# Gate and up products of a feed-forward layer: a 512-column matmul over both halves of the activations, the halves summed by VectorE

## The reference

```python
D_FF = 2816
def swiglu(u, w_gu, w_down):                 # u 256 x 1024, w_gu 1024 x 5632, w_down 2816 x 1024
    gate, up = jnp.split(u @ w_gu, 2, axis=-1)
    return (jax.nn.silu(gate) * up) @ w_down
...
        u = rmsnorm(x, ffn_pre_g[i])
        x = x + rmsnorm(swiglu(u, ffn_w_gu[i], ffn_w_down[i]), ffn_post_g[i])
```

## Time and profile before

| | us |
|---|---|
| median of 3 runs (960.03 to 960.82) | 960.06 |
| the profiled execution, its own time | 959.71 |
| its span, first to last instruction | 957.9 |
| PE busy in the span | 925.8 |
| DVE busy in the span | 568.7 |
| ACT busy in the span | 482.9 |
| granted TensorE clock, mean (1 is 2.4 GHz) | 0.989 |

### The profile page before, as it was taken

One profiled execution on the slowest core, in us unless ns is written; L12 is line 12 of the kernel. 1 busy time (PEld: TensorE's weight loads), 2 busy tenths in 40 slices (PEclk: granted clock), 3 DMA queues, 4 the chain that ended last, 5 costly groups with the idle time before them and its releaser, 6 DMA issues.

```text
span 957.9 us, 15627 instructions
## 1 busy us (share of the span) xinstructions
PE 925.8 (97%) x6624; PEld 858.1 (90%) x6624; DVE 568.7 (59%) x645; ACT 482.9 (50%) x654; POOL 55.2 (6%) x67
## 2 busy tenths in 40 slices
PE   8999999999999989999999999999999599999996
PEld 7999998878898889999988999987998499999885
DVE  6788466895755655554543854665844745554533
ACT  6566467763645554444434644666544544444332
POOL 1000003450000000000000220000000000000000
PEclk9999999999999999999999999999999799999999
DMA  8856444235642565555555796424652355555551
GB/s 264 267 189 190 144 148 138 90 91 193 207 169 88 180 204 187 175 175 178 191 202 176 238 271 207 132 100 132 222 172 91 110 167 184 175 175 178 201 192 44
DMA packets 121061, 163.80 MB, mean 171 GB/s; under 512 B 4076, under 2 KB 106916, under 8 KB 121012
## 3 DMA queue, kind: packets, MB, share of 16 engines
q1 hardware_dynamic: 117684, 151.99, 49.0%
q0 software_dynamic: 3328, 11.10, 3.8%
HBM read 162.01 MB, written 1.07 MB: 170 GB/s over the span
## 4 chain that ended last, share of the span: by engine, by line
PE 83%; DVE 10%; ACT 4%; issue 2%; DMA 1%; SPq 0%; DVEq 0%; POOL 0%; ACTq 0%; POOLq 0%
PE bank L449 75%; DVE w_lo L1148 2%; DVE ntmp L1211 1%; PE bank L756 1%; PE bank L727 1%; DVE x L1214 1%; DVE ntmp L1190 1%; ACT ntmp L867 1%; PE bank L645 1%; PE bank L551 1%; DMA d_pair<-in_ssm_d_dram 1%; DVE stats L1179 1%; DVE stats L1181 1%; PE bank L811 1%; DMA pre_row<-in_kv_norm_g_dram 1%
## 5 line engine op out<-in xcount | busy, mean ns | idle before, releaser
L1148 DVE TENSOR_TENSOR w_lo<-w_raw,w_hi 128x2048 fp32r<-128x2048 f32 x135 | 309.1, 2294 | 215.2 <-ACT w_hi L845 215.1
L449 PE MATMUL bank<-actT_hi,w_hi 128*128 128x256 f32 x1280 | 365.5, 286 | 3.6 <-DVE actT_lo L1198 1.6
L449 PE MATMUL bank<-actT_lo,w_hi 128*128 128x256 f32 x1280 | 363.8, 284 | 0.0
L449 PE MATMUL bank<-actT_hi,w_lo 128*128 128x256 f32 x1280 | 363.7, 284 | 0.0
L845 ACT ACTIVATE w_hi<-w_raw 128x2048 fp32r<-128x2048 f32 x135 | 256.7, 1907 | 94.7 <-DMA w_raw<-in_ffn_w_down_dram 52.8
L449 PEld LDWEIGHTS bank<-actT_hi,w_hi 128*128 128x128 f32 x1280 | 246.9, 193 | 5.8 <-issue 5.0
L449 PEld LDWEIGHTS bank<-actT_lo,w_hi 128*128 128x128 f32 x1280 | 246.9, 193 | 0.1
L449 PEld LDWEIGHTS bank<-actT_hi,w_lo 128*128 128x128 f32 x1280 | 246.9, 193 | 0.0
L449 PE MATMUL bank<-w_hi,hT_hi 128*128 128x512 f32 x176 | 68.6, 390 | 0.0
L449 PE MATMUL bank<-w_lo,hT_hi 128*128 128x512 f32 x176 | 68.6, 390 | 0.0
L449 PE MATMUL bank<-w_hi,hT_lo 128*128 128x512 f32 x176 | 68.5, 389 | 0.0
(11 more groups left out here) (209 smaller groups left out, 1293.1 us busy)
## 6 DMA issues: line engine op xcount, KB each, us to landing
w_raw<-in_ffn_w_gu_dram SPq DMA_DIRECT2D x44, 1024.0 KB, 5.1
w_raw<-in_ffn_w_down_dram SPq DMA_DIRECT2D x22, 1024.0 KB, 4.9
w_raw<-in_ssm_w_in_dram SPq DMA_DIRECT2D x20, 1024.0 KB, 5.4
w_raw<-in_mem_w_kv_dram SPq DMA_DIRECT2D x16, 1024.0 KB, 5.5
w_raw<-in_ssm_w_out_dram SPq DMA_DIRECT2D x8, 1024.0 KB, 5.0
w_raw<-in_mem_w_q_dram SPq DMA_DIRECT2D x8, 1024.0 KB, 5.4
w_raw<-in_mem_w_o_dram SPq DMA_DIRECT2D x8, 1024.0 KB, 5.0
w_raw<-in_w_kv_dram SPq DMA_DIRECT2D x8, 1024.0 KB, 5.6
```

The costliest lines, as they stand in the source:

```text
L449: ins = pe.matmul(dst, a, b, start=first and n == 0, stop=last and n == len(passes) - 1, skip_group_check=True)
L1148: dve.tensor_tensor(lo[:, s, :], raw[:, s, :], hi[:, s, :].bitcast(F32), ALU.subtract).then_inc(w_lo_done, 1)
```

## The change

- `actT_hi` and `actT_lo` become the two planes of one tensor `actT` [128, 8, 2, 256], so that for each k the high and the low half lie side by side.
- PE: gate and up units go through a new `pair_unit`. For each c and k it issues one matmul of 512 columns (high weights with both halves of `actT[k]`) and one of 256 columns (low weights with the high half), the latter added onto columns 256 to 511. Each c has a bank of its own: columns 0 to 255 hold hi·hi, columns 256 to 511 hold hi·lo + lo·hi. Units alternate between banks 0, 1 and banks 2, 3.
- DVE: for every unit a `tensor_reduce` reads the two banks (1024 values on each partition, viewed so that the two halves of an output are the inner dimension, 256 values apart) and writes 512 sums, to `gate` for an even unit and to `hval` for an odd one. It frees the banks. The multiplication by gate then reads and writes `hval` in SBUF.
- ACT: silu reads `gate` in SBUF, in place, after DVE's sum (new semaphore `gate_ready` tells DVE); the copy to `hT_hi` waits for `h_ready`. `w_hi` is made for unit j+3, and one unit more is split ahead of the first pass.

```diff
     if name in ("gu0", "gu1"):
-        return "dve" if i % 2 else "act"
+        return "dve"
...
-        actT_hi = place("actT_hi", [P, KD, S], F32R)
-        actT_lo = place("actT_lo", [P, KD, S], F32R)
+        actT = place("actT", [P, KD, 2, S], F32R)
+        actT_hi, actT_lo = actT[:, :, 0, :], actT[:, :, 1, :]
...
+            def pair_unit(slot, b):
+
+                for c in range(2):
+                    for k in range(KD):
+                        cols = slice(k * TC + c * P, k * TC + (c + 1) * P)
+                        wh, wl = hi[:, slot, cols], lo[:, slot, cols]
+                        pe.matmul(bank[:, b + c, :], wh, actT[:, k].rearrange("p e n -> p (e n)"), start=k == 0, stop=False,
+                                  skip_group_check=True)
+                        ins = pe.matmul(bank[:, b + c, S:2 * S], wl, actT_hi[:, k, :], start=False, stop=k == KD - 1,
+                                        skip_group_check=True)
+                return ins
...
                 with pe.Fori(0, iters) as i:
                     for j in range(5):
                         if j:
-                            e, n = free_of_slot(j, i)
-                            pe.wait_ge(t_out[e], n)
+                            pe.wait_ge(t_out["dve"], i * 4 + (d0 + j - 1))
                         if j < 4:
                             pe.wait_ge(w_lo_done, i * 4 + (u0 + j + 1))
-                            t_unit((u0 + j) % SLOTS, (v0 + j) % 2, actT_hi, actT_lo).then_inc(w_used, 1)
+                            pair_unit((u0 + j) % SLOTS, j % 2 * 2).then_inc(w_used, 1)
...
 # ScalarE
-                    hi_unit(u0 + 2 + j, i, per)
-                    act.wait_ge(w_used, i * 4 + (u0 + j + 1) if per else u0 + j + 1)
+                    hi_unit(u0 + 3 + j, i, per)
                     if j % 2 == 0:
-                        act.activation(gate[:, j // 2 % 2], tiles((v0 + j) % 2), ACT.Silu).then_inc(t_out["act"], 1)
+                        act.wait_ge(t_out["dve"], i * 4 + (d0 + j + 1) if per else d0 + j + 1)
+                        act.activation(gate[:, j // 2 % 2], gate[:, j // 2 % 2], ACT.Silu).then_inc(gate_ready, 1)
                     else:
-                        act.wait_ge(t_out["dve"], i * 2 + (d0 + j // 2 + 1) if per else d0 + j // 2 + 1)
+                        act.wait_ge(h_ready, i * 2 + (g0 + j // 2 + 1) if per else g0 + j // 2 + 1)
                         act.activation(hT_hi[:, tile, :], hval[:, j // 2 % 2], ACT.Copy).then_inc(h_hi, 1)
...
-            hi_upto(U[("gu0", 0)] + 1)
+            hi_upto(U[("gu0", 0)] + 2)
...
 # VectorE
                     lo_unit(u0 + 2 + j, i, per)
+                    b = j // 2 % 2
+                    halves = bank[:, j % 2 * 2:j % 2 * 2 + 2, :].rearrange("p c (e n) -> p c n e", e=2)
+                    dst = hval if j % 2 else gate
+                    dve.wait_ge(w_used, i * 4 + (u0 + j + 1) if per else u0 + j + 1)
+                    dve.tensor_reduce(dst[:, b], halves, AX.X, ALU.add).then_inc(t_out["dve"], 1)
                     if j % 2:
-                        b = j // 2 % 2
-                        dve.wait_ge(w_used, i * 4 + (u0 + j + 1) if per else u0 + j + 1)
-                        dve.wait_ge(t_out["act"], i * 2 + (a0 + j // 2 + 1) if per else a0 + j // 2 + 1)
-                        dve.tensor_tensor(hval[:, b], tiles((v0 + j) % 2), gate[:, b], ALU.mult).then_inc(t_out["dve"], 1)
+                        dve.wait_ge(t_out["dve"], i * 4 + (d0 + j + 1) if per else d0 + j + 1)
+                        dve.wait_ge(gate_ready, i * 2 + (h0 + j // 2 + 1) if per else h0 + j // 2 + 1)
+                        dve.tensor_tensor(hval[:, b], hval[:, b], gate[:, b], ALU.mult).then_inc(h_ready, 1)
                         dve.wait_ge(h_hi, i * 2 + (h0 + j // 2 + 1) if per else h0 + j // 2 + 1)
                         dve.tensor_tensor(hT_lo[:, tile, :], hval[:, b], hT_hi[:, tile, :].bitcast(F32), ALU.subtract).then_inc(h_lo, 1)
```

More of the change, by code:

```diff
@@ L307, in program @@
         h_hi, h_lo = sem("h_hi"), sem("h_lo")
+        gate_ready, h_ready = sem("gate_ready"), sem("h_ready")
         stored = sem("stored")
@@ L480, in banked @@
                 pe.wait_ge(w_lo_done, u + 1)
+                if name in ("gu0", "gu1"):
+                    pair_unit(u % SLOTS, i % 2 * 2).then_inc(w_used, 1)
+                    return
                 f = t_unit if KIND[name] == "T" else v_unit
@@ L498, in fill_half, with loop_t @@
                     ins.then_inc(w_used, 1)
-            def loop_t(name, iters, free_of_slot):
+            def loop_t(name, iters):
                 u0, v0 = U[(name, 0)], V_OF[(name, 0)]
+                d0 = FREED[v0][1] - 1
                 for e, n in FREED[v0 - 2:v0]:
@@ L765, in feed_forward @@
                 name = f"gu{layer}"
-                a0, d0 = FREED[V_OF[(name, 0)]][1] - 1, FREED[V_OF[(name, 1)]][1] - 1
-                loop_t(name, 5, lambda j, i: (("act", "dve")[j % 2], i * 2 + ((a0, d0)[j % 2] + j // 2)))
+                loop_t(name, 5)
                 for i in (20, 21):
@@ L1060, in feed_forward @@
                 u0, v0 = U[(name, 0)], V_OF[(name, 0)]
-                a0, d0 = FREED[v0][1] - 1, FREED[v0 + 1][1] - 1
+                d0, g0 = FREED[v0][1] - 1, (FT // 2) * layer
                 act.preload_act_table_set("silu_and_others")
                 def unit(j, i, per, tile):
-                    hi_unit(u0 + 2 + j, i, per)
-                    act.wait_ge(w_used, i * 4 + (u0 + j + 1) if per else u0 + j + 1)
+                    hi_unit(u0 + 3 + j, i, per)
                     if j % 2 == 0:
-                        act.activation(gate[:, j // 2 % 2], tiles((v0 + j) % 2), ACT.Silu).then_inc(t_out["act"], 1)
+                        act.wait_ge(t_out["dve"], i * 4 + (d0 + j + 1) if per else d0 + j + 1)
+                        act.activation(gate[:, j // 2 % 2], gate[:, j // 2 % 2], ACT.Silu).then_inc(gate_ready, 1)
                     else:
-                        act.wait_ge(t_out["dve"], i * 2 + (d0 + j // 2 + 1) if per else d0 + j // 2 + 1)
+                        act.wait_ge(h_ready, i * 2 + (g0 + j // 2 + 1) if per else g0 + j // 2 + 1)
                         act.activation(hT_hi[:, tile, :], hval[:, j // 2 % 2], ACT.Copy).then_inc(h_hi, 1)
@@ L1078, in feed_forward @@
                     unit(j, 0, 0, slice(FT - 2, FT))
-                done[0] = u0 + 24
+                done[0] = u0 + 25
                 m_part(f"down{layer}")
@@ L1133, in _ @@
             turn(7, actT_hi)
-            hi_upto(U[("gu1", 0)] + 1)
+            hi_upto(U[("gu1", 0)] + 2)
             feed_forward(1)
@@ L1403, in feed_forward @@
                 name = f"gu{layer}"
-                u0, v0 = U[(name, 0)], V_OF[(name, 0)]
-                a0 = FREED[v0][1] - 1
+                u0 = U[(name, 0)]
+                d0 = FREED[V_OF[(name, 0)]][1] - 1
                 h0 = (FT // 2) * layer
```

## The result

The changed kernel takes 955.02 us, the median of 5 runs (952.92 to 955.59), against 960.03 us before (959.69 to 960.82). The ratio is 0.9945, with a 95% interval of 0.9935 to 0.9956: faster by 0.55%. The forecast was 950.7 us with a range of 948.8 to 954.5, so the direction held and the size didn't: 5.0 us came where 9.3 were expected, and the median lies outside the range. The profiled execution (954.65 us) has a span of 952.8 us, 5.1 less than before.

What follows compares the result with a forecast made beforehand. PE's matmul stream in the two feed-forward layers was taken as the bound. From 959.71 us, 9.3 us of PE saving (9.4 less 0.1 at low clock) gave 950.4, plus 0.35 to the median: 950.7 us, range 948.8 to 954.5.

Steps and rivals of the forecast that it cites:

- The bound: Both feed-forward layers: PE's own stream sets the time, number of matmuls times distance between starts; PE waits for nothing.
- The cost of a matmul: Gate and up units: 13.3 ns beside the columns at either width; one 512 for two 256 saves 13.4 ns, 9.4 us over 704 steps.
- The bounds for this term: PE's saving per gate and up step: not under 0, at most 26.7 ns if the 256-column matmul's 13.3 ns hid too.
- the 357 from which the prediction called itself wrong: Gate and up stretch: a distance of 357 ns or more between 512-column matmuls would prove the prediction wrong; 346.6 expected.
- Rival 1: PE's gate and up steps: less of the fixed part is saved, 2.5 ns a step, 1.8 us in all: 958.3 us; chance 0.03.
- Rival 3: Layer edges: late loads or ACT splits, or a sum of 1.6 to 2.1 us, make PE wait: 953 to 956 us; chance 0.06.
- rival 2: DVE becomes the bound: strided sum at 2.35 us, round 11.8 us, +6.4 us, about 966 us; chance 0.06.
- Rival 4: PE's gate and up steps: the 256-column matmul's fixed part hides too, twice the saving: 941 us; chance 0.02.
- DVE: DVE's new sum takes about 1.24 us; its round of two units, 9.4 us, fits under PE's 11.1, so PE doesn't wait.
- ACT's lead: ACT splitting one unit further ahead in gate and up: no price, as PE never waits for `w_hi` or `w_lo`.
- No gain either: ACT one unit ahead saves no time by itself, but DVE no longer idles before its splits, where the sums go.
- Loads, layout, the way into the down projection: Loads at 189 GB/s in place of 183, interleaved `actT`, and PE going on to the down projection: nothing added.

Runs made afterwards that it cites:

- three of 256: Changed kernel with the 512-column matmul undone into two of 256 columns (high weights with each half), the rest kept: 960.67 us, ratio 1.0002.
- two of 512: Changed kernel with the low weights too multiplied with both halves, so every gate and up matmul has 512 columns: 1025.71 us.
- the same weights: Changed kernel with the 256-column matmul using the high weights in place of the low ones; widths, order and columns kept: 954.49 us.
- eight of 512 ahead: Changed kernel with eight further matmuls of 512 columns ahead of each layer's loop, into a bank cleared afterwards: 954.12 us.
- runs of sixteen: Changed kernel with each unit's sixteen 512-column matmuls first, then its sixteen 256-column ones: 952.26 us, ratio 0.9913.

## Why the prediction was wrong, step by step

**The bound.** Right. The gate and up stage is PE's own stream before and after, with no wait of PE in it.

**The cost of a matmul: the step that failed.** The prediction put a step at 226.6 + 120.0 = 346.6 ns and its saving at 13.4 ns, "at which both widths were measured". Both widths had been measured, but each in a stream of its own. The two figures are exact there (120.0 and 226.6 ns again, with three of 256 and with two of 512), but alternating they add up only in one of two rhythms. In the other, which both layers of the profiled execution had, a step is 353.3 ns and saves 6.7: 704 x 6.7 = 4.7 us in place of 9.3. The 4.6 us that are missing account for the whole of the 4.3 us by which the median lies above the forecast; the 0.4 us of a shorter stretch at the low clock are part of the rest. The bounds for this term, 0 to 26.7 ns a step, did contain it. The fault after that was in the range: an untested mix of two widths was given an error of 1 ns a step, where its own bounds allowed 13, and the stretch from 954.5 to 958 was left almost empty. The measured 353.1 ns also lies between the forecast's 346.6 and the 357 from which the prediction called itself wrong.

**The rivals of the prediction.** Rival 1 had the right place (part of the 13.3 ns stays) and the wrong reason: it named the turn from high to low weights, which the same weights rule out, and its 958.3 us went too far. Rival 3 (953 to 956 us) has the measured 955.0 in its range, but by luck: it named waits of PE at the edges of the layers, and the two that there are, 1.0 and 1.6 us at the starts, stood in the kernel before as well. Its sum of 1.6 to 2.1 us also doesn't agree with rival 2, by which nothing is lost up to 2.0. Rival 4, a fixed part that hides altogether, came the other way round.

The page "TensorE: Matmul & The Clock Gate" of the Trainium skill (section "Back-to-back issue gap") gives 2.5 ns beside the columns for an isolated matmul, and says that in a stream the weight loads count too. The prediction held the 2.5 ns against a stream. These streams of one width show 13.3, and with mixed widths 13.3 or 16.7 ns, on average of both widths.

**DVE.** Right, and tested: the sum takes 1.22 us, DVE's round fits under PE's, and with the widths undone the rest of the change has ratio 1.0002. Rival 2, the strided read, did not come. The rule on PSUM lines that stood behind it, of the page "PSUM — Partial Sum Buffer" of the Trainium skill (section "Specifications (TRN2)"), is about matmuls. This read by DVE, at 1.22 us where the values' number alone gave 1.24, pays nothing for its stride of 256 values.

**ACT's lead.** The trace after agrees that it has no price: ACT's idle time moved to its wait for loads, 48.8 us in the stretch shown. "No gain either" was wrong for the change as a whole. The prediction did say that the lead makes the room where the sums go, but it set no price on that room. PE waited for no split before, but before no sum stood in the chain from one split to the next. With the sums and a lead of two the chain takes 12.8 us a pair and the kernel 2% more than before. The lead isn't an addition to this change, it is what makes the rest of it free.

**Loads, layout, the way into the down projection.** As predicted, nothing; loads run at 184 GB/s in the stretch shown.

**What stays open.** What inside PE makes the two rhythms isn't known. The runs show that the slow one doesn't come from the columns written or the memory of the weights, and that neither the operands nor the other engines' new work cost anything without mixed widths. They suggest, with few profiles, that the way into the stream chooses. They don't show why the slow one has a period of three steps, or whether a way in can be made that always gives the fast one for less than it costs. The fast rhythm in both layers was seen only with eight of 512 ahead, never with nothing ahead.

## What to carry to other kernels

Price a matmul by the distance between starts in a stream like the one that it will stand in; two widths measured apart need not add up when they alternate, and where a sum allows any order, long runs of one width are the safe one (here 0.9907 to 0.9917 of the time before, against 0.9935 to 0.9945; some of these intervals overlap, and it is the unit times that tell the orders apart: 5.56 to 5.59 us in long runs, 5.65 or 5.55 in turn, by the rhythm). An operation put into a loop of two engines belongs to every chain that passes through it: before calling a lead worthless, add up the chain without it.

## What the runs showed of the hardware

- At the granted clock 1.00, a stream of matmuls of one width, each with its weight load, costs its columns at 2.4 per ns plus 13.3 ns: 120.0 ns for 256 columns and 226.6 for 512. At the 1.2 GHz level the 13.3 ns don't show (0.21 us for 256).
- 512 and 256 columns in turn run at either 346.7 or 353.3 ns a step for hundreds of steps. The same program had the one in its second layer in one execution and the other in the next.
- A single change of width between long runs costs 10 ns on average of the two directions. In the runs of sixteen the first five distances of the wide ones are 228 to 236 ns and the later ones 227; the first two of the narrow ones are 113 and 119 ns and the later ones 120.
- A reduction on DVE of 1024 fp32 values in PSUM to 512 results, the two values of each 1 KB apart, takes 1.22 us. Against the 0.69 us of 512 adjacent values that is 1.05 ns for each further value, no more than side by side (1.08 to 1.09 between the two reductions of the earlier trace rows), so the stride costs nothing.
